# Second block: the first pair of differential scores and its softmax ahead of the feeds of the banded queries, keys and values

## The reference, cut to what matters

```python
    proj = h @ w_in
    c_q, c_kv, k_r, d_q, d_k, d_v, s_q, s_k, s_v, gate_logits = jnp.split(proj, offs, axis=-1)
    ...
    dq = rms_norm(d_q.reshape(b, s, 2, DIFF_HEADS, DIFF_QK), g_diff_q)
    dk = rms_norm(d_k.reshape(b, s, 2, DIFF_HEADS, DIFF_QK), g_diff_k)
    ...
        s = jnp.einsum('bqmhd,bkmhd->bmhqk', qb, k, preferred_element_type=jnp.float32) * scale
        dist = jnp.abs(pb[:, :, None] - pos_f[:, None, :])
        s = s - slopes[None, None, :, None, None] * dist[:, None, None]
        p = jax.nn.softmax(s, axis=-1)
    ...
    wq = rms_norm(s_q.reshape(b, s, WIN_HEADS, WIN_HEAD_DIM), g_win_q)
    wk = rms_norm(s_k.reshape(b, s, WIN_KV_HEADS, WIN_HEAD_DIM), g_win_k)
    wv = s_v.reshape(b, s, WIN_KV_HEADS, WIN_HEAD_DIM)
    gates = jax.nn.sigmoid(gate_logits.reshape(b, s, N_BRANCH, D_MODEL))
```

## Time and profile before

| | |
|---|---|
| median of 3 runs | 1748.23 us (1746.33 to 1748.44) |
| the profiled execution's own time | 1745.46 us |
| its span | 1743.6 us |
| mean granted TensorE clock | 0.987 |
| TensorE busy | 96% of the span |
| VectorE, ScalarE, GpSimd busy | 67%, 53%, 25% |

### The profile page before, as it was taken

How to read it: one execution, slowest core, us unless ns; L and a number is a source line. 1 busy time by engine, 2 the same in 40 slices (tenths; PEclk the granted TensorE clock), 3 DMA queues, 4 the chain that set the end, 5 groups by cost and what they waited for, 6 DMA issues and landing times.

```text
span 1743.6 us, 30149 instructions
## 1 busy us (share of the span) xinstructions
PE 1670.2 (96%) x11354; PEld 1520.1 (87%) x11354; DVE 1172.7 (67%) x1609; ACT 920.7 (53%) x1576; POOL 443.6 (25%) x184
## 2 busy tenths in 40 slices
PE   8989999999989999999999999999899999999997
PEld 6878799988887899978899989999788999899996
DVE  5687754458786644476784777666758856777667
ACT  5654544446645544465655564444665555554445
POOL 2212222212222222224511122222235211222222
PEclk9989999999999999999999999999999999999999
DMA  8432455556423655546323455665464333566653
GB/s 329 154 122 91 150 201 181 190 160 208 155 77 115 229 181 182 182 144 227 125 97 111 134 190 183 209 196 177 150 214 156 106 101 115 172 205 199 203 179 126
DMA packets 82563, 288.74 MB, mean 166 GB/s; under 512 B 9051, under 2 KB 11908, under 8 KB 81924
## 3 DMA queue, kind: packets, MB, share of 16 engines
q1 hardware_dynamic: 77352, 272.58, 47.7%
q10 hardware_dynamic: 5084, 14.37, 2.4%
HBM read 284.81 MB, written 2.11 MB: 165 GB/s over the span
## 4 chain that ended last, share of the span: by engine, by line
PE 62%; DVE 7%; ACT 2%; issue 2%; DVEq 0%; ACTq 0%
PE bank L716 30%; PE bank L733 25%; DVE w_lo L682 2%; PE bank L1287 2%; PE bank L1268 1%; PE bank L1259 1%; PE bank L761 1%; PE bank L1247 1%; ACT w_hi L678 1%; PE bank L1300 0%; DVE qk L2513 0%; PE bank L906 0%; PE bank L1179 0%; PE bank L914 0%; DVE z L2105 0%
## 5 line engine op out<-in xcount | busy, mean ns | idle before, releaser
L682 POOL TENSOR_TENSOR w_lo<-raw,w_hi 128x1024 fp32r<-128x1024 f32 x146 | 376.6, 2579 | 1225.6 <-ACT w_hi L678 1225.6
L682 DVE TENSOR_TENSOR w_lo<-raw,w_hi 128x1024 fp32r<-128x1024 f32 x364 | 555.9, 1551 | 155.2 <-ACT w_hi L678 153.8
L678 ACT ACTIVATE w_hi<-raw 128x1024 fp32r<-128x1024 f32 x510 | 519.9, 1051 | 107.3 <-PE bank L716 47.4
L716 PE MATMUL bank<-x_t_hi,w_hi 128*128 128x256 f32 x1984 | 326.7, 287 | 5.5 <-ACT gl L1423 3.0
L716 PE MATMUL bank<-x_t_lo,w_hi 128*128 128x256 f32 x1984 | 319.8, 284 | 0.0
L716 PE MATMUL bank<-x_t_hi,w_lo 128*128 128x256 f32 x1984 | 319.5, 283 | 0.0
L716 PEld LDWEIGHTS bank<-x_t_hi,w_hi 128*128 128x128 f32 x1984 | 279.0, 192 | 18.0 <-issue 5.7
L716 PEld LDWEIGHTS bank<-x_t_lo,w_hi 128*128 128x128 f32 x1984 | 274.5, 192 | 0.0
L716 PEld LDWEIGHTS bank<-x_t_hi,w_lo 128*128 128x128 f32 x1984 | 274.3, 192 | 0.0
L733 PE MATMUL bank<-w_hi,x_t_hi 128*128 128x512 f32 (+3 forms) x448 | 134.5, 383 | 9.1 <-issue 5.8
L733 PE MATMUL bank<-w_hi,x_t_lo 128*128 128x512 f32 (+3 forms) x448 | 131.5, 376 | 1.5 <-DVE x_t_lo L1946 1.5
(11 more groups left out here) (391 smaller groups left out, 2134.5 us busy)
## 6 DMA issues: line engine op xcount, KB each, us to landing
raw<-stream SPq DMA_DIRECT2D x511, 512.0 KB, 4.3
rows<-rows ACTq DMA_DIRECT2D x4, 1024.0 KB, 4.7
gain<-rows ACTq DMA_DIRECT2D x8, 512.0 KB, 4.2
hv_p<-hv_dram ACTq DMA_DIRECT2D x14, 256.0 KB
x<-x_in SPq DMA_DIRECT2D x2, 512.0 KB, 4.9
bias_r<-rev_dram SPq DMA_DIRECT2D x1, 1024.0 KB, 7.3
hv_dram<-hv ACTq DMA_DIRECT2D x2, 512.0 KB, 6.9
y_out<-x SPq DMA_DIRECT2D x2, 512.0 KB, 2.7
```

What stands on the lines that cost most here:

```text
L678: self.eng.activation(w_hi[:, i, :], raw[:, i, :], ACT.Copy).then_inc(hi_done.sem, 1)
L682: self.eng.tensor_tensor(w_lo[:, i, :], raw[:, i, :], w_hi[:, i, :].bitcast(F32), ALU.subtract).then_inc((lo_pool if self.part == "pool" e ...
L716: mm = pe.matmul(target, a[:, i, w0 + kt * P:w0 + (kt + 1) * P], b[:, k0 + kt, :], start=kt + k == 0, stop=k == 2 and kt == kts - 1)
```

## The change

The scores of items 0 and 1 are issued on TensorE before the feeds of `sq` and `skv` instead of behind them. DVE's two items 0 and 1 are issued before its remainders of units 25, 27 and 28 (`split.ahead(uid["sq3"])`), and ACT's two exponentials before its roundings of units 25 to 28. The loop skips them. The instructions are the same in kind and number.

```diff
+                pe.wait_ge(*banks.read(at, "dqt0"))
+                pe.wait_ge(*banks.read(at, "dqt1"))
+                scores_pair(0)
                 pe.wait_ge(*banks.free(at, "sq"))
                 feed([f"sq{k}" for k in range(4)], x_t_hi, x_t_lo, pair_of(0, 512), 2, 512, ["sq"])
                 pe.wait_ge(*banks.free(at, "skv"))
                 feed([f"skv{k}" for k in range(4)], x_t_hi, x_t_lo, pair_of(2, 256), 2, 256, ["skv"])
...
-                    if i < MLA and i % 2 == 0:
+                    if 0 < i < MLA and i % 2 == 0:
                         scores_pair(i)
...
+                item_exp2(0)
+                item_exp2(1)
                 split.ahead(uid["sq3"])
                 head_squares(at, "sq", 3, 0, 512)
                 head_norms(at, 3, 16)
...
                 for i in range(ITEMS + 2):
-                    if i < ITEMS:
-                        act.wait_ge(*c["z_ready"](at, i + 1))
...
+                    if 2 <= i < ITEMS:
+                        item_exp2(i)
...
-                split.ahead(uid["sq3"])
-                head_means(at, 3, 8)
-                head_scale(at, "sq", 3, 8, 0, sqn)
-                split.ahead(uid["skv3"])
-                head_means(at, 4, 2)
-                head_scale(at, "skv", 4, 2, 2, skn)
-
                 def item(i):
...
+                item(0)
+                item(1)
+                split.ahead(uid["sq3"])
+                head_means(at, 3, 8)
+                head_scale(at, "sq", 3, 8, 0, sqn)
+                split.ahead(uid["skv3"])
+                head_means(at, 4, 2)
+                head_scale(at, "skv", 4, 2, 2, skn)
+
```

More of the change, by code:

```diff
@@ L1221, in second_block @@
                                 ).then_inc(*banks.fills(at, f"ukv{t}"))
[L1222 to L1225, removed]
                 def scores_pair(i):
@@ L1250, in scores_pair @@
                                 mm.then_inc(*banks.fills(at, f"s{i + half}"))
+                pe.wait_ge(*banks.read(at, "dqt0"))
+                pe.wait_ge(*banks.read(at, "dqt1"))
+                scores_pair(0)
+                pe.wait_ge(*banks.free(at, "sq"))
+                feed([f"sq{k}" for k in range(4)], x_t_hi, x_t_lo, pair_of(0, 512), 2, 512, ["sq"])
+                pe.wait_ge(*banks.free(at, "skv"))
+                feed([f"skv{k}" for k in range(4)], x_t_hi, x_t_lo, pair_of(2, 256), 2, 256, ["skv"])
                 def scores2(i):
@@ L1301, in mla_turn @@
                     mm.then_inc(*banks.fills(at, f"mt{n}"))
-                pe.wait_ge(*banks.read(at, "dqt0"))
-                pe.wait_ge(*banks.read(at, "dqt1"))
                 for i in range(ITEMS + 3):
-                    if i < MLA and i % 2 == 0:
+                    if 0 < i < MLA and i % 2 == 0:
                         scores_pair(i)
@@ L1764, in second_block, with item_exp2 @@
                                ).then_inc(c["qk_act"].sem, 1)
+                def item_exp2(i):
+                    act.wait_ge(*c["z_ready"](at, i + 1))
+                    for t in range(T):
+                        source, scale = ((z2[:, i % 4, t * S:(t + 1) * S], 1.0) if i < MLA else
+                                         (bank[banks.bank(at, f"s{i}")][:, t * S:(t + 1) * S], MLA_SCALE))
+                        ins = act.activation(z2[:, i % 4, t * S:(t + 1) * S], source, ACT.Exp, scale=scale,
+                                             bias=neg_max[:, stat_of(i) + t:stat_of(i) + t + 1],
+                                             accum_out=sums2[:, stat_of(i) + t:stat_of(i) + t + 1])
+                    ins.then_inc(c["p_ready"].sem, 1)
+                    if i >= MLA:
+                        act.wait_ge(*c["p_ready"](at, i + 1))
+                        act.nop().then_inc(*banks.frees(at, f"s{i}"))
+                item_exp2(0)
+                item_exp2(1)
                 split.ahead(uid["sq3"])
```

## The result

| | before | after |
|---|---|---|
| median | 1746.53 us (16 runs) | 1751.49 us (16 runs) |
| after to before | | 1.0025, 95% interval 1.0018 to 1.0032 |
| the profiled execution's own time | 1745.46 us | 1753.74 us |
| its span | 1743.6 us | 1752.0 us |

The change makes the kernel 0.25% slower, 4.4 us by the ratio (0.0025 x 1746.5). The medians lie 5.0 us apart. The forecast was +1.3 us and 1749.5 us, with 75% on a change within the 0.2% that the prediction took as its line; by that line the result is its case "slower", which had 12%. The measured median lies inside the range, near its upper end.

A forecast was written before the change was run, and what follows sets the result against it. TensorE, busy 96% of the span, was taken to bound the kernel, losing time only when idle or at lower clock. Two layers x 0.65 us gave +1.3 us on the median: 1749.5 us, range 1745.0 to 1752.8.

The forecast's parts named there:

- case "slower": Whole kernel: slower than before by over 0.2% (3.5 us); chance 12%.
- rival B: TensorE before `gl2`: the clock falls in layer 1 too, costing 1.50 us; +2.8 us in all, 1751.0 us; chance 25%.
- C: TensorE, both layers: the lower clock lasts about twice as long; +5.8 us, 1754.0 us; chance 9%.
- The reading of the holes and their cause: TensorE at the loop start: three holes, 3.26 us a layer, because VectorE and ScalarE come late to items 0 and 1.
- The block put on ScalarE: ScalarE waits until 821.8 us for its exponentials ahead of four roundings; unit 28 rounded at 828.0, 2.1 us late.
- The turns between VectorE and GpSimd: Remainders and `mla_sq` on the two engines exclude each other; the sum of squares of `sq` starts 4.8 us late.
- Rival D: VectorE and GpSimd: their remainders don't disturb each other; `gl2` 3.2 us earlier, 1741.8 us; chance 2%.
- The walk: Step-by-step timing of layer 0 across the engines, ending with `gl2` 0.65 us later than before.
- What follows from 4.8 us: Chain behind the late sum of squares: `gl0` read 1.65 us later, one exponential's 1.0 us regained, `gl2` 0.65 us later.
- cover: Slack for delayed remainders, costed at nothing: 3.6 us for unit 28's before `gl1`, 3.9 us for unit 26's before `skv` ends.
- TensorE at either place 1.1 us: TensorE: the eight matmuls of the first scores take 1.1 us at the old or new place, so `gl1` still ends at 840.0.
- The sum: Both layers of the second block: 2 x 0.65 us = +1.3 us at an unchanged clock, giving 1749.5 us.

The follow-up runs named there:

- experiment 2: Changed kernel with ScalarE's two exponentials behind its roundings of units 25 to 28 instead of ahead: 0.9963 of the kernel before, median 1739.69 us.
- experiment 3: Changed kernel with GpSimd's `mla_sq` of tile 1 ahead of its remainder of unit 26: 0.9979 of the kernel before, median 1742.09 us.
- experiment 9: Changed kernel with first scores between feeds of `sq` and `skv`, items between units 29 and 31, exponentials behind squares of `skv`: 0.9961 of before, 1740.08 us.
- experiment 5: Changed kernel with VectorE's items and ScalarE's exponentials laid between the weight steps of units 25 to 28: 0.9978 of the kernel before.
- experiment 1: Kernel before with only TensorE's part of the change, first scores ahead of the feeds: 1.0035 of the kernel before, median 1751.75 us.
- 8: Changed kernel run again unchanged, on the chip of other follow-up runs: 1.0020 of the kernel before, median 1751.76 us.
- 12: Changed kernel run unchanged a third time, beside the one with both holes filled: 1.0023 of the kernel before, median 1751.18 us.
- experiment 4: Changed kernel with 24 thrown-away matmuls a layer in TensorE's hole behind the second scores: 1.0013 of the kernel before, median 1748.42 us.
- 11: Changed kernel with both holes filled by thrown-away matmuls, 28 behind the second scores and 4 before `gl2`: 1.0007 of before, median 1748.14 us.

## Why the prediction was right, and where it was not

**The number** lies in the range with some luck. It was set on the median of 3 runs, 1748.23 us; over 16 runs the kernel before has 1746.53, which is 1.7 us less. Against its own kernel the change costs 4.4 us by the ratio and 5.0 by the medians, and the range's upper end allowed 4.6 (1752.8 - 1748.2). That is between rivals B (+2.8) and C (+5.8).

**The reading of the holes and their cause** was right. Experiments 2, 3 and 9 move `gl2` by moving nothing but VectorE's, GpSimd's and ScalarE's orders (and the place of the first scores), and by the amounts worked out, to within 0.15 us.

**The block put on ScalarE** was right, and experiment 2 shows it to be the step that loses the gain: with it `gl2` is 0.68 us later than before, without it 2.69 us earlier.

**The turns between VectorE and GpSimd** were right for the changed kernel, to 0.1 us, and their price is shown by experiment 3. Rival D (no disturbance) is out: three VectorE remainders took 6.99 us in experiment 2. The walk is delicate, though: experiment 5 turned the order of the turns over by a shift of 0.3 us and lost nearly 2 us a layer.

**"What follows from 4.8 us"** held: 1.65 us late at `gl0`, 0.65 predicted and 0.68 measured at `gl2`. No cover failed. Two small readings are off and leave `gl2` where it is: the second scores start 0.24 us earlier than the 840.0 of the prediction, and rival B counts the four transposes as 0.44 us where the earlier trace rows show 0.63. So the holes are 3.68 and 0.50 us, not 3.4 and 0.7.

**"TensorE at either place 1.1 us"** was right for TensorE, but the prediction gave no price for what the move does to the feed of `sq`. In the changed kernel it has none, since VectorE's lateness is longer; alone it costs 1.0 us a layer (experiment 1), and experiment 9 avoids it: its sum of squares of `sq` starts 12.69 us behind the copy, where that of experiment 2 starts at 14.09 and that of before at 12.64. How much of the 0.76 us a layer between 9 and 2 this makes is not shown apart.

**The term that was mis-sized is the clock.** The sum took the clock as unchanged: +1.3 us. Measured are 4.4 us, of which the steps make 1.4; with the holes filled 1.2 us are measured, so some 3 us are the lower clock behind a longer hole. Rival B had the mechanism, for one layer more, with 25% and +2.8 us. In the three profiled executions of the changed kernel (after, 8 and 12) `gl2` took 3.85 to 4.47 us in both layers, not in one of them. Beyond `gl2` the trace after has another such stretch in each layer, at the feeds behind the last softmax, where the windows of before (948 to 980 and 1440 to 1470 us) have a granted clock of 1.00. Windows of the trace after; the third number from the end is the granted clock:

```profile
968.50:972.00 3.50, 3.39 (x20) 2.99 (x21) 1.47 (x3) 3.50 (x8) 0.00 (x0) 0.63 0.12 44
1460.00:1463.60 3.60, 3.43 (x19) 3.15 (x20) 1.43 (x4) 3.59 (x8) 0.00 (x0) 0.63 0.16 59
```

The traces show what these stretches cost. From the start of `gl2` to the first matmul with `hs_hi` (line 733), 1478 matmuls further on, it is 198.5 us where no lower clock falls between (198.55 in layer 1 of before, 198.54 in both layers of experiment 4). In the trace after it is 200.14 and 199.86 us. `gl2` alone makes 1.44 and 1.24 of the excess (4.42 and 4.22 instead of 2.98), so the later stretch costs 0.1 to 0.2 us a layer. It is there in all six layers of the changed kernel's three traces, and also in 6 of the 22 layers of the other eleven traces, the kernel before with its holes filled among them; whether the change makes it more frequent stays open. Experiments 8 and 12 have one lower stretch more in layer 0, at that `hs_hi` feed (in 8 at 1049.0 to 1052.4 us, granted 0.50, two matmuls of 128x512 in 1.05 us instead of 0.63), and it costs 1.5 us. What brings it on is not shown.

From `gl2` on, the lower clock thus costs 2.9, 3.6 and 4.3 us in the traces of after, 8 and 12, of which 2.7, 1.7 and 2.6 at `gl2`, against 1.5 us in before and 0.1 or less in 4 and 11. That is enough for the 2.3 to 3.0 us that the filling takes off, and most of it in two of the three traces, about half in the third, lies at `gl2`.

## What to carry to other kernels

A piece moved ahead on an engine with a fixed list puts a wait ahead of everything behind it: ask when its input is ready, and put it behind the work that is ready earlier. Four exponentials exchanged with four roundings on ScalarE made the difference between 4.4 us slower and 4.9 to 6.5 us faster. Where two engines take turns at something, look for the time in which one stands in line, and fill it with work that does not need the turn. Price a hole on TensorE with the clock that follows it: here the clock cost more than the hole had grown.

## What the runs showed of the hardware

VectorE's and GpSimd's instructions with two SBUF inputs held each other up for whole instructions. When both were in line they took turns one by one: VectorE's units 27 and 28 took 6.36 us in the changed kernel, with the end of GpSimd's remainder ahead of the first and `mla_sq` between them. When VectorE was not in line, GpSimd ran two in a row, and VectorE's 1.1 us took 3.52 (experiment 5). VectorE's distance terms and maxima (one input in PSUM, or one input only) ran beside GpSimd's remainder undisturbed: 0.68 and 0.69 us in experiment 9, as in the other traces. The Trainium skill, "GPSIMD Engine Reference", Specifications, names two SBUF inputs as a case of contention; the rows agree.

Useless matmuls made a kernel faster: 32 a layer took 3.0 us off the changed kernel's median, with the mean granted clock up from 0.9838 to 0.9875. TensorE's idle time in this place had grown by 0.9 us a layer, 1.8 us in both (4.18 against 3.26); the clock behind it cost more than that.
